# Two-block language-model kernel: the decay matrices of the first mixer masked by TensorE, exponentiated per head by ScalarE, and group roots kept in accumulator memory

## The reference, cut to what matters

```python
# 4 groups of 8 heads, head size 64, state 128, two chunks of 128 tokens
a_cs = cumsum(dt * a)                                    # per head, inside a chunk
xdt = x * dtc[..., None]
decay = exp(where(causal, a_cs[..., :, None] - a_cs[..., None, :], -inf))
cb = einsum('bclgn,bcsgn->bcgls', cc, bc)
y_diag = einsum('bcgrls,bcsgrp->bclgrp', cb[:, :, :, None] * decay, xdt)
states = einsum('bclgn,bcgrl,bclgrp->bcgrpn', bc, exp(a_cs[..., -1:] - a_cs), xdt)
y_off = einsum('bclgn,bcgrpn,bcgrl->bclgrp', cc, prev, exp(a_cs))
y = y_diag + y_off + xs * d_skip[:, None]
yz = y * silu(z)                                         # z: 2048 columns of the input projection
yz = yz * rsqrt(mean(yz * yz, axis=-1) + EPS)            # over each group's 512 columns
out = (yz * norm_g) @ w_out
```

## Time and profile before

| | us |
|---|---|
| median of 3 runs (range) | 1995.33 (1993.35 to 1996.22) |
| the profiled execution, its own time | 1991.34 |
| its span, first to last instruction | 1989.6 |
| TensorE busy over the span | 1774.5 (89%) |
| VectorE busy over the span | 1186.2 (60%) |
| mixer core, first cb product to the end of the last group's y | 121.36 to about 231 |
| y scaled, first transposes for the output projection | 250.91 |
| second of the 8 output units begins | 261.19 |

### The profile page before, as it was taken

How to read it: one execution, slowest core, us unless ns; L and a number is a source line. 1 busy time by engine, 2 the same in 40 slices (tenths; PEclk the granted TensorE clock), 3 DMA queues, 4 the chain that set the end, 5 groups by cost and what they waited for, 6 DMA issues and landing times. The chain is left out here.

```text
span 1989.6 us, 34679 instructions
## 1 busy us (share of the span) xinstructions
PE 1774.5 (89%) x12455; PEld 1652.0 (83%) x12455; DVE 1186.2 (60%) x2351; ACT 788.9 (40%) x997; POOL 913.2 (46%) x268
## 2 busy tenths in 40 slices
PE   5888599999996799998865689979999999999996
PEld 5887599999995699998644689979999988888885
DVE  6769936444284354447578579084555547777775
ACT  3543324334552243333320344444444443333332
POOL 4652356888681048885400248896666630000000
PEclk9987899999895699998855799999999999999998
DMA  4432234555451025555200136654555577777774
GB/s 169 149 109 83 85 107 167 181 183 190 148 188 46 1 86 191 190 190 175 88 19 0 53 111 221 232 198 154 175 182 177 175 256 237 238 237 238 237 238 147
DMA packets 77436, 310.84 MB, mean 156 GB/s; under 512 B 8752, under 2 KB 10288, under 8 KB 60720
## 3 DMA queue, kind: packets, MB, share of 16 engines
q1 hardware_dynamic: 74288, 304.64, 45.5%
q10 hardware_dynamic: 3072, 5.15, 0.8%
HBM read 290.89 MB, written 18.87 MB: 156 GB/s over the span
## 5 line engine op out<-in xcount | busy, mean ns | idle before, releaser
L700 POOL TENSOR_TENSOR lo<-raw,hi 128x2048 fp32r<-128x2048 f32 x128 | 589.6, 4617 | 561.1 <-ACT hi L542 487.8
L336 PE MATMUL ps<-xh,hi 128*128 128x256 f32 (+1 forms) x1984 | 570.4, 287 | 40.0 <-POOL lo L700 22.1
L337 PE MATMUL ps<-xl,hi 128*128 128x256 f32 (+1 forms) x1984 | 561.5, 283 | 0.0
L338 PE MATMUL ps<-xh,lo 128*128 128x256 f32 (+1 forms) x1984 | 561.5, 283 | 0.0
L336 PEld LDWEIGHTS ps<-xh,hi 128*128 128x128 f32 x1984 | 379.5, 191 | 44.1 <-issue 32.2
L719 POOL TENSOR_TENSOR lo<-raw,hi 128x1024 fp32r<-128x1024 f32 x128 | 321.2, 2536 | 138.8 <-ACT hi L1492 138.8
L338 PEld LDWEIGHTS ps<-xh,lo 128*128 128x128 f32 x1984 | 379.1, 191 | 0.0
L337 PEld LDWEIGHTS ps<-xl,hi 128*128 128x128 f32 x1984 | 378.5, 191 | 0.2
L1492 ACT ACTIVATE hi<-raw 128x1024 fp32r<-128x1024 f32 x256 | 264.6, 1057 | 214.7 <-PE ps L338 204.7
L2121 DVE TENSOR_TENSOR lo<-raw,hi 128x1024 fp32r<-128x1024 f32 x128 | 156.2, 1222 | 86.4 <-ACT hi L1492 86.3
L336 PE MATMUL ps<-hi,wgh 128*128 128x512 f32 x512 | 201.1, 393 | 1.2 <-DVE wgl L2132 1.2
(11 more groups left out here) (436 smaller groups left out, 3331.7 us busy)
## 6 DMA issues: line engine op xcount, KB each, us to landing
raw<-in_w_u SPq DMA_DIRECT2D x128, 512.0 KB, 4.2
raw<-in_w_v SPq DMA_DIRECT2D x128, 512.0 KB, 4.2
raw<-in_w_up SPq DMA_DIRECT2D x44, 1024.0 KB, 4.8
raw<-in_w_down SPq DMA_DIRECT2D x22, 1024.0 KB, 4.7
raw<-in_w_fox SPq DMA_DIRECT2D x16, 1024.0 KB, 4.9
act_save<-act_out SPq DMA_DIRECT2D x64, 256.0 KB, 2.0
act_in<-act_save SPq DMA_DIRECT2D x64, 256.0 KB, 3.2
raw<-in_w_xbc SPq DMA_DIRECT2D x12, 1024.0 KB, 4.9
```

Source lines behind the costliest of these rows:

```text
L336: pe.matmul(o, ah, bh, start=start, stop=False)
L337: pe.matmul(o, ah, bl, start=False, stop=False)
L338: return pe.matmul(o, al, bh, start=False, stop=stop)
L700: return g.tensor_tensor(lo[slot][:], raw[slot][:], hi[slot][:].bitcast(F32), ALU.subtract)
```

## The change

Four things are changed together, and nothing outside the mixer.

1. `rowbc` first writes the causal mask into banks 4 and 5 by one bf16 matmul each (`negm`, 0 or -1e30, against a repeated identity), and the eight head sums are accumulated onto it. ScalarE takes the exponential out of the banks head by head, with the negative of the row's own sum as bias. The eight VectorE subtractions, `cbm` and its semaphore go; VectorE multiplies `dec` by cb straight from bank 2.
2. `xdt` is made once for all groups in eight pieces, from banks 2 and 3, in the convolution part (`make_xdt`), instead of two times in each group. `xs_turn` waits for a piece before it writes its bank again.
3. `scale_group` takes the roots of both chunks in one chain of eleven small instructions, with the middle value of each pass in bank 3 (the last group: bank 0), and signals `y_ready` for each group.
4. The output projection starts as soon as three groups are scaled; its fifth of eight column blocks waits until the last y has been taken from banks 6 and 7 (`y_added`). The last addition, gate and scaling come between `dve_out`'s pieces.

```diff
-    def pe_w(pe, s, bh, bl, first_k, last_k):
+    def pe_w(pe, s, bh, bl, first_k, last_k, after_y=False):
...
+            if after_y and c == 4:
+                pe.wait_ge(y_added, 8)
...
         def fill(n):
+            if groups:
+                pe.wait_ge(y_ready, 1 if n == 0 else max(3, n // 2 + 1))
...
+            if v >= 2:
+                pe.wait_ge(xdt_made, v - 1)
...
                 if i >= 1:
-                    pe.wait_ge(row_min, i)
-                for r in range(HPG):
-                    hd = g * HPG + r
-                    m = pe.matmul(ps[:, 4 + r // 4, (r % 4) * P:(r % 4 + 1) * P],
-                                  dtv[:, 1, c, hd:hd + 1].broadcast_to([P, P]), tri[:], start=True, stop=True)
+                    pe.wait_ge(dec_ready, i)
+                for q in range(2):
+                    pe.matmul(ps[:, 4 + q, :], negm[:, T2 - P:], bc(identb[:], 1, [P, 4, P]), start=True, stop=False)
+                    for r in range(4 * q, 4 * q + 4):
+                        hd = g * HPG + r
+                        m = pe.matmul(ps[:, 4 + q, (r % 4) * P:(r % 4 + 1) * P],
+                                      dtv[:, 1, c, hd:hd + 1].broadcast_to([P, P]), tri[:], start=False, stop=r % 4 == 3)
                 m.then_inc(row_mm, 1)
...
             def exps(i):
-                act.wait_ge(row_min, i + 1)
-                sig_a(s.activation(dec[i % 2][:], dec[i % 2][:], ACT.Exp), dec_ready)
+                g, c = CORE[i]
+                act.wait_ge(row_mm, i + 1)
+                if i >= 2:
+                    act.wait_ge(y_mm, i - 1)
+                for r in range(HPG):
+                    hd = g * HPG + r
+                    ins = s.activation(dec[i % 2][:, r, :], ps[:, 4 + r // 4, (r % 4) * P:(r % 4 + 1) * P], ACT.Exp,
+                                       bias=dtv[:, 10, c, hd:hd + 1])
+                sig_a(ins, dec_ready)
...
+            def make_xdt(n):
+
+                v.wait_ge(xs_evac, n + 2)
+                sig_v(v.tensor_tensor(xdt[:, :, n * 256:(n + 1) * 256].rearrange("p t (a b) -> p t a b", a=4),
+                                      ps[:, 2 + n % 2, :].rearrange("p (t a b) -> p t a b", t=2, a=4),
+                                      dtv[:, 0, :, 4 * n:4 * n + 4].unsqueeze(3).broadcast_to([P, NT, 4, HD]), ALU.mult), xdt_made)
...
                 sig_v(ins, xbc_conv)
+                if u >= 6:
+                    make_xdt(u - 6)
             v.wait_ge(acs_e, 1)
-            v.wait_ge(xs_evac, 9)
-
-            def scale_group(g):
+            make_xdt(6)
+            make_xdt(7)
+
+            def scale_group(g, bank):
+                v.wait_ge(g_ssq, 2 * g + 2)
+                r = stat[:, 24 + 2 * g:26 + 2 * g]
+                rsqrt(v, ch, r, stat[:, 16 + 2 * g:18 + 2 * g], 512, rs[:, 0, 0:2], ps[:, bank, 0:2], rs[:, 2, 0:2])
                 for c in range(NT):
-                    i = 2 * g + c
-                    v.wait_ge(g_ssq, i + 1)
-                    rsqrt(v, ch, stat[:, 24 + i:25 + i], stat[:, 16 + i:17 + i], 512)
                     yg = y_tm[:, c, g * 512:(g + 1) * 512]
-                    ch(v.tensor_scalar(yg, yg, stat[:, 24 + i:25 + i], None, ALU.mult))
+                    ins = v.tensor_scalar(yg, yg, r[:, c:c + 1], None, ALU.mult)
+                sig_v(ins, y_ready)
...
+            def gate_and_scale(n):
+                if n == 2:
+                    add_y(2 * GROUPS - 1)
+                    gate_group(GROUPS - 1)
+                if n == 3:
+                    scale_group(GROUPS - 1, 0)
...
-                for r in range(HPG):
-                    a_s = dtv[:, 6, c, g * HPG + r:g * HPG + r + 1]
-                    ins = v.tensor_scalar(dec[i % 2][:, r, :], ps[:, 4 + r // 4, (r % 4) * P:(r % 4 + 1) * P], a_s, a_s, ALU.min, ALU.subtract)
-                sig_v(ins, row_min)
...
-                sig_v(v.tensor_tensor(dec[i % 2][:], dec[i % 2][:], bc(cbm[:, c, :], 1, [P, HPG, P]), ALU.mult), m_ready)
+                v.wait_ge(cb_mm, g + 1)
+                sig_v(v.tensor_tensor(dec[i % 2][:], dec[i % 2][:], bc(ps[:, 2, c * P:(c + 1) * P], 1, [P, HPG, P]), ALU.mult), m_ready)
```

More of the change, by code:

```diff
@@ L499, in chain_mark, with pe_out @@
         sig_v(v.memset(stat[:, 127:128], 0.0), s)
[L502 removed]
+    def pe_out(pe, src, nv, u0, done0, groups=False):
         def fill(n):
+            if groups:
+                pe.wait_ge(y_ready, 1 if n == 0 else max(3, n // 2 + 1))
             if n >= 2:
@@ L516, in pe_out, with dve_out @@
             pe.wait_ge(o_ready, done0 + n + 1)
-            pe_w(pe, (u0 + n) % RING, oh[:, n % 2], ol[:, n % 2], n == 0, n == nv - 1)
-    def dve_out(v, nv, gain, u0, done0):
+            pe_w(pe, (u0 + n) % RING, oh[:, n % 2], ol[:, n % 2], n == 0, n == nv - 1, groups and n == 0)
+    def dve_out(v, nv, gain, u0, done0, between=None):
         for n in range(nv):
+            if between is not None:
+                between(n)
             v.wait_ge(o_filled, done0 + n + 1)
@@ L806, in y_diag @@
                     pe.wait_ge(y_added, i)
+                g, c = CORE[i]
                 for r in range(HPG):
-                    m = pe.matmul(ps[:, 6, r * HD:(r + 1) * HD], dec[i % 2][:, r, :], xdt[i % 2][:, r, :], start=True, stop=True)
+                    hd = g * HPG + r
+                    m = pe.matmul(ps[:, 6, r * HD:(r + 1) * HD], dec[i % 2][:, r, :], xdt[:, c, hd * HD:(hd + 1) * HD], start=True, stop=True)
                 m.then_inc(y_mm, 1)
-                g, c = CORE[i]
                 if c == 1:
@@ L814, in y_diag, with cb @@
                     pe.matmul(ps[:, 7, :], bct[:, GROUPS + g, P:2 * P], st_t[:], start=True, stop=True).then_inc(yoff_mm, 1)
[L816 to L821, removed]
+            def cb(g):
                 for c in range(NT):
@@ L825, in ssd @@
                 m.then_inc(cb_mm, 1)
-                for i in (2 * g, 2 * g + 1):
-                    rowbc(i)
-                    if i >= 1:
-                        y_diag(i - 1)
-                    z_unit(i)
-                    if i == 2 * g:
-                        pe.wait_ge(xdst_ready, g + 1)
-                        if g >= 1:
-                            pe.wait_ge(st_ready, g)
-                        pe.matmul(ps[:, 3, :], b_tm[:, g, :], xdst[:].rearrange("p a b -> p (a b)"),
-                                  start=True, stop=True).then_inc(st_mm, 1)
+            pe.wait_ge(xs_evac, 9)
+            pe.wait_ge(xdt_made, 8)
+            pe.wait_ge(xbc_silu, 12)
+            for i, (g, c) in enumerate(CORE):
+                rowbc(i)
+                if i >= 1:
+                    y_diag(i - 1)
+                if c == 0:
+                    cb(g)
+                z_unit(i)
+                if c == 0:
+                    pe.wait_ge(xdst_ready, g + 1)
+                    if g >= 1:
+                        pe.wait_ge(st_ready, g)
+                    pe.matmul(ps[:, 3, :], b_tm[:, g, :], xdst[:].rearrange("p a b -> p (a b)"),
+                              start=True, stop=True).then_inc(st_mm, 1)
             y_diag(7)
-            pe.wait_ge(y_ready, 1)
-            pe_out(pe, y_tm, 8, U_SOUT, 0)
+            pe_out(pe, y_tm, 8, U_SOUT, 0, groups=True)
         def ffn(l, u0):
```

34 lines of the change are left out of this document (13 added, 21 removed).

## The result

The changed kernel takes 1962.43 us (median of 4 runs, 1957.52 to 1965.01) where the kernel before, run beside it, takes 1995.78 us (4 runs, 1993.35 to 1996.48): a ratio of 0.9832, interval 0.9811 to 0.9853. It is faster by 33.4 us, 6.6 us short of the 40.0 predicted: inside the stated range of 1948 to 1967, but outside the 1950 to 1961 that the prediction gave its likeliest case. The profiled execution took 1962.6 us, 28.7 less than that of before.

A forecast was written before the change was run, and what follows sets the result against it. VectorE was taken to bound the core at 30.16 us a group, TensorE afterwards at 21.6. With the ends, output transposes moved from 261.19 to 221.2, gaining 40.0 us: 1995.33 - 40.0 = 1955, range 1948 to 1967.

The forecast's parts named there:

- likeliest case: Whole kernel: TensorE bounds the core as summed, 1950 to 1961 us, chance 0.72.
- some 8.2 us: Core, each 30.16 us VectorE period: two small root instructions stand still for GpSimd's subtractions; the other 22.0 are work.
- Counting it again: Core, per group: 8.5 us of GpSimd holds added again to VectorE's 12.5 us of work, 21.0 at most.
- 0.6 us of slack: Core, per group: product with cb ready at 13.6, wanted by TensorE at 14.2, the tightest place.
- the start of the core: TensorE begins 0.75 us later, plus 1.3 for four masks: second z unit ends at 144.4 instead of 142.37.
- warning about small instructions: ScalarE's eight exponentials: each pays fixed latency, tiles should have at least 512 elements; estimated 2.0 us, ScalarE staying under TensorE.
- The last gate falls beside the first unit's end: Output projection: last gate beside first unit's end, last scaling beside the second, delaying nothing; later units take what they took.
- the y wait: Inside the first output unit: half through at 217.1, it waits for the last y until 218.3, about 1 us.
- The hold longer than the slack: Core: GpSimd's hold makes the product with cb 1 to 4 us late per group; 1958 to 1967 us, chance 0.17.
- The half clock: Core: recurring TensorE waits add about 7 us per group, 1977; chance 0.09 shared with VectorE staying on the path.
- VectorE still on the path: Core: slower `dec` products or `xdt` pieces delaying the convolution, 1981 us; chance 0.09 shared with the clock case.
- Slower by the exponentials: ScalarE, core: per-head exponentials decide the period above 0.71 us each, slower kernel from 1.54; chance 0.02.

The follow-up runs named there:

- masks_three: Changed kernel with each of the sixteen mask matmuls issued three times, the first two results overwritten: 1970.41 us, ratio 0.9884 to the kernel before.
- dve_decay: Changed kernel with part 1 undone (no masks on TensorE, VectorE subtracts again), parts 2 to 4 kept: 1970.34 us, ratio 0.9875 to the kernel before.
- exps_twice: Changed kernel with six of eight exponentials of each step taken a second time into an unread tile: 1966.57 us, ratio 0.9854 to the kernel before.
- before: The kernel without the change, run beside the others as reference: 1995.78 us.
- after: The changed kernel, all four parts, against the kernel without them: 1962.43 us, ratio 0.9832.
- scale_later: Changed kernel with the last group's two scalings moved one output piece later, its roots left in place: 1959.34 us, ratio 0.9833 to the kernel before.
- early_mark: scale_later, with the mark that frees banks 6 and 7 given before the third addition of y: 1953.5 us, ratio 0.9791 to the kernel before.
- after_again: The changed kernel a second time, unedited: 1960.3 us, ratio 0.9832 to the kernel before.
- before_overlap: The kernel before with part 4, the early output projection, alone: 1992.24 us, ratio 0.999 to the kernel before.

## Why the prediction was right, and what was mis-sized

**The bound.** Right: VectorE's 30.16 us period was replaced by TensorE's 21.5 (predicted 21.6). masks_three shows by its 1.7 us a group that TensorE decides, dve_decay that without part 1 VectorE would still, at 26.9.

**What VectorE was held for.** The step said that of each period "some 8.2 us" are VectorE standing still. They were, but a hold is no cost that goes away with the instruction that shows it. Taking the roots out gave 2.46 us a group, and the full 8.5 us is still in the changed kernel. Counting it again was right. It was laid out a little short: behind the z unit's end GpSimd's two subtractions end at 189.44 + 9.59 - 189.06 = 9.97 in the last group, where the sum had 8.6. That used up the 0.6 us of slack. That the period held all the same is in part luck: 1.6 us more of ScalarE's work a step (exps_twice) were enough for a wait of 2.2 us there.

**The single costs.** Mask 0.22 us (0.24), exponential 0.27 (2.18/8; predicted 0.33, bound above 0.367), the start of the core 1.0 us better than summed. The last was luck: the sum kept the first z unit of before, which began at half clock and took 132.27 - 125.65 = 6.62 us; in after it runs at the full clock throughout, 135.46 - 129.69 = 5.77. The Trainium skill's warning about small instructions (VectorE: DVE Perf Modes, The TRN2 errata) did not decide. It is stated for instructions that read SBUF, and these read the accumulator memory. Eight exponentials of 128 columns take 2.18 us against 1.06 for one of 1024, near the 2.0 us estimated from its figure, and ScalarE had the room. How little more it had, exps_twice shows.

**The ends: the step that failed.** "The last gate falls beside the first unit's end, the last scaling beside the second, and they delay nothing." They delay. VectorE takes its instructions in order, and the last root and scaling took 4.40 and 4.55 us (rows above), where 0.17 and 0.88 are usual, with the rounding of the fourth output piece behind them. TensorE waited 2.82 us for `ol` (L540) and then ran at a granted clock of 0.76, so that 10.66 us lie between transposes (238.13 to 248.79) where 6.0 is usual: 4.6 us. scale_later takes 4.4 to 4.9 us of it back. The second place is the y wait, "about 1 us" in the prediction and 218.3 - 217.1 = 1.2 in its sum: it was 2.56, 1.4 more, because one addition was held (2.29 where 0.69 is usual), and the clock behind it was 0.62, so that the other half of the unit took 4.47 us where the sum had 2.9: another 1.6 us. With some 0.4 of small terms the first output unit came 3.4 us late. early_mark takes back 4.0.

**The account.** Predicted 40.0, less 4.6 and 3.4, plus 1.0 for the start of the core: 33.0 in the stretch, which is what 231.0 - 198.0 measures, and near the median gain of 33.4. The profiled gain is 28.7: less 2.5 for the prefix sums, which began at 70.3 instead of 67.8 us, and 1.8 for everything behind the stretch. Both lie in the spread of the profiles. The prefix sums begin at 67.9 us in after_again, the same kernel, and at 67.8 to 71.7 in the others. Behind the stretch it is 1690.8 us in before, 1692.6 in after and 1687.5 to 1695.6 in the others; a piece of that, the attention (from the first to the last transpose of its queries, the same code in all), takes 74.6 us in before and 78.1 in after and after_again, and 72.8 to 78.1 in the others, three of them with the change at 74.6.

**The rivals.** The hold longer than the slack cost only some 0.1 us in the groups, and 7 to 8 us at the ends. This was the rival given 0.17, for 1958 to 1967, and the measured 1962.4 is inside the stated range only because it was widened for it: the right mechanism, but at a place that the likeliest case called free. The half clock did not recur per group (1.00 in the core). VectorE still on the path: no; the last transposes of x waited for a piece of `xdt`, but 5.51 us, where before they waited 5.39 for ScalarE. Slower by the exponentials: 0.27 us is far from 1.5.

## What to carry to other kernels

When the bound moves from a waiting engine to a working one, the gain inside the loop can be summed from the distances between starts, and here came within 0.1 us a group; the hand-overs cannot. There, list for each engine the instructions in order, and for each in-order neighbour that is not on the path ask what stands behind it. A held instruction tells whom it waits for, not what can be saved: before paying for its removal, look which instruction would be held next. And an idle TensorE costs twice, once for the wait and once for the clock behind it; filling 2.8 us of wait won 3.9.

## What the runs showed of the hardware

- A root instruction of one word that reads one SBUF tile ran in 0.15 us beside GpSimd's subtraction, and so did the first one of a chain (`rs<-stat`, at 255.45 us in before_overlap, where GpSimd subtracts from 255.21 on); this first one with two words took 4.40 us in after (L431, above), and 0.17 in the core, with GpSimd idle. Scalings of 512 columns were held as well: 4.55 us for a pair that takes 0.88. The prediction had named only instructions with two SBUF tiles as sure. The Trainium skill (SBUF — State Buffer, Who interferes with whom) has it that a scaling in a two-port mode is held too; the trace agrees, with these numbers. That one word escapes and two do not fits what the Trainium skill (VectorE: DVE Perf Modes, Mode 2×_2P) asks of this mode, operands in SBUF whose outermost dimension of more than one element is even, or odd and equal in source and destination; no run here tried other counts.
- In after, waits of 2.56 and 2.82 us were followed by 4.5 and 7.2 us at a mean granted clock of 0.62 and 0.76, against 1.00 ahead of each; one of 1.61 us (at 216.05) and one of 0.26 us (early_mark) were followed by 1.00.
- The same code differs between profiles by up to 3.9 us at the start (67.8 to 71.7) and 5.3 us in the attention (72.8 to 78.1). Two profiles of the changed kernel had stretches of 198.0 and 198.5 us, where the times of one kernel's runs ranged over 2 to 10 us.
